# Three of the eleven down-projection units as seven block products each, with their sums and low parts on VectorE

## The chip, the cores and the metric

The kernel runs on one core of one Trainium2 chip. The metric is the device time of one execution in microseconds (us), as the median of several runs. The engines are TensorE (PE in the profile; PEld is its weight load), VectorE (DVE), ScalarE (ACT), GpSimd (POOL) and SyncE (SP), which issues most of the DMAs. SBUF is the working memory of all of them; PSUM (the tile `ps`, eight banks of 128x512) takes the matmul results and is read by ACT and DVE.

## What is computed

Two decoder layers on 256 tokens with a width of 1024. The change touches one product in each layer, that of the gated MLP with the down weights (2816x1024):

```
for i in range(DEPTH):                      # DEPTH = 2
    ...
    x = x + groups.reshape(B, S, MIX_WIDTH) @ w_o[i]
    h = rms_norm(x, ffn_norm[i])
    u = causal_depthwise_conv(h @ w_up[i], conv_w[i], conv_b[i])
    x = x + (jax.nn.silu(u[..., :D_FF]) * u[..., D_FF:]) @ w_down[i]
    x = x + (p[i] @ ple_proj[i]) * jax.nn.sigmoid(x @ ple_gate[i])
```

## The kernel before

**Split numbers.** Every large product is made from numbers split in two: a high part (the value rounded to the matmul format `fp32r` by a copy) and a low part (value minus high part). `split_product` (L963, L964, L965) issues three matmuls: high by high, high by low, low by high.

**Units.** The weights come as units of 128x2048 numbers (1 MB), some of half that. Each layer has 10 units of the input projection, 5 of `w_o`, one of `ple_proj`, 22 of `w_up`, 11 of `w_down` (`U_DOWN` + 0 to 10, here down 0 to down 10) and 5 of `ple_gate` (`U_GATE` + n, here gate 0 to 4). A unit passes through these steps, each engine doing its own in the order in which the code writes them:

- SP loads it into one of `DEEP` = 6 slots of `raw` when the unit six places earlier has been used (`w_used`, which PE raises after the last matmul of a unit).
- ACT copies it to the high part (`high`, L590) in one of `RING` = 3 buffers `wh`, when the unit three places earlier has been used.
- Someone subtracts the high part for the low part `wl`: POOL for everything from up unit 2 to the end of the layer (`low`, L461), DVE for the earlier ones (L1724).
- PE uses it, in the order of the units.

**The down stage.** The activation of step s (256 of the 2816 rows, so `STEPS` = 11 steps) is made during the up stage: DVE multiplies (`product`, L2082), ACT copies the high part (`product_high`, L894) and DVE subtracts (`product_low`, L2087) into `g_high(s)` and `g_low(s)`, which lie in `gT_h`, `gT_l` and `g_late`. For the two token tiles of 128 and the two halves of 512 columns, down unit s adds two products of depth 128 into one of the banks 0 to 3 (`wide`). That is 8 block products, or 24 matmuls of 128x512. When down 10 finishes a bank, `add_to_x` (L2041) on DVE adds the bank to one of the four quarters of `x` and signals `x_mlp`.

**After it.** PE waits for `x_mlp` quarter by quarter, transposes the quarter (`x_T`, L1015), ACT copies the high part (`x_high`, L604), DVE the low part (`x_low`, L1673), and PE begins gate 0 (L1539, L1541), whose first matmul waits for two of the four high parts. ACT makes the high parts of gate 0 and gate 1 before `x_high`, those of gate 2 to 4 after it; POOL makes their low parts.

A line of the profile is a line of the kernel; many lines belong to helpers.

Of the kernel before, what the change touches and what calls it, by code (L numbers as in the profile page):

```python
# [7 lines left out]
F32 = mybir.dt.float32  # L8
# [7 lines left out]
P = 128  # L16
# [40 lines left out]
DEEP = 6  # L57
# [18 lines left out]


def unit_up(s, half):

    return U_FFN + 2 * s + half  # L80
# [25 lines left out]
def _cols(n):  # L106
# [34 lines left out]
    "wo_done": 3, "x_mid": 4, "low_copied": 2 * STEPS, "halves_summed": 2 * STEPS, "tap2": 4 * STEPS, "tap1": 4 * STEPS, "conv_done": 4 * STEPS,  # L141
    "silu": STEPS, "prod": STEPS, "g_high": STEPS, "g_low": STEPS, 
    "proj_done": 3, "pp_ready": 4, "down_done": 3, "x_mlp": 4, "gate_ready": 3, "sigmoid": 4, "ple_term": 4,
# [30 lines left out]
def build(nc, x_in, p_cols, positions, w_in, w_uq, w_ukv, attn_cols, norm_gains,  # L174
          small_gains, w_o, w_up, conv_cols, w_down, ple_proj, ple_gate, out):
    with ExitStack() as ctx:
# [26 lines left out]
        with nc.sbuf_tensor("proj_h", [P, SLOT], F32R) as proj_h:  # L203
            pass
        hT = sb("hT", [P, KT, SEQ])
        hT_hl = sb("hT_hl", [P, KT * 2 * SEQ + UP_AT], F32R)
# [3 lines left out]
        sb("hT_edge", [P, 32])  # L210
        gT_h = sb("gT_h", [P, 2, 2, SEQ], F32R)
        gT_l = sb("gT_l", [P, 2, 2, SEQ], F32R)
# [19 lines left out]
        pT = sb("pT", [P, 2, SEQ])  # L232
        pT_h = sb("pT_h", [P, 2, SEQ], F32R)
        ng = sb("ng", [P, 2 * D])
        with nc.sbuf_tensor("uq_l", [P, 2, H * QK], F32R) as uq_l:
# [60 lines left out]
        def g_low(s):  # L296
            return gT_l[:, s] if s < EARLY else g_late[:, 1, s - EARLY]

        def mixed(high, g):
# [67 lines left out]
        def ffn_lows(layer, u):  # L367

            return layer * (UNITS - U_POOL) + (u + 1 - U_POOL)

# [47 lines left out]
        def _(pool):  # L418
# [36 lines left out]
            for layer in range(DEPTH):  # L455
# [101 lines left out]
                pool.wait_ge(F["hn_ready"], base["hn_ready"] + 4)  # L557
                for u in range(U_POOL, UNITS):
                    low(u)
# [6 lines left out]
        def _(act):  # L566
# [7 lines left out]
            for layer in range(DEPTH):  # L574
# [316 lines left out]
                def product_high(s):  # L891
# [3 lines left out]
                                   ).then_inc(F["g_high"], 1)  # L895

                act.wait_ge(F["conv_landed"], base["conv_landed"] + 16)
                high(U_FFN + 2)
                for s in range(STEPS):
                    low_half(s, 0)  # L900
                    high(unit_up(s, 0) + 3)
                    if s:
                        product_high(s - 1)
                    if s > 1:
                        act.wait_ge(F["g_low"], base["g_low"] + s - 1)
# [15 lines left out]
                if layer + 1 < DEPTH:  # L921
                    act.wait_ge(F["g_low"], base["g_low"] + STEPS)
                    latent_high(pt_r, M_MLA_B, layer + 1, "mla_high")
                    latent_high(pb_r, M_MLA_A, layer + 1, "mla_a_high")
# [14 lines left out]
        def _(pe):  # L939
# [6 lines left out]
            for layer in range(DEPTH):  # L946
                base = before(layer)
                def unit(u):

                    if u in WHOLE:  # L950
                        pe.wait_ge(raw_landed[u % DEEP],
                                   (layer * (UNITS // DEEP) + u // DEEP + 1) * 16)
                    elif u == U_WO:
                        pe.wait_ge(F["out_low"], layer + 1)
                    elif u < U_POOL:
                        pe.wait_ge(l_made, lows(layer, u))
                    else:
                        pe.wait_ge(ffn_l_made, ffn_lows(layer, u))
                    return u % DEEP, w_high(u)
# [565 lines left out]
                pe.wait_ge(F["conv_done"], base["conv_done"] + 4 * (STEPS - 1))  # L1525
                for s in range(STEPS):
                    pe.wait_ge(F["g_low"], base["g_low"] + s + 1)
                    wide(U_DOWN + s, 2, 0, g_high(s), g_low(s), s == 0, s == STEPS - 1,
                         name="down_done" if s == STEPS - 1 else None)
# [50 lines left out]
        def _(dve):  # L1580
# [64 lines left out]
            for layer in range(DEPTH):  # L1645
# [431 lines left out]
                def product(s):  # L2077

                    g = cv[s % 2][:, 0:2, :]
                    dve.wait_ge(F["silu"], base["silu"] + s + 1)  # L2080
                    dve.wait_ge(F["conv_done"], base["conv_done"] + s * 4 + 4)
                    tt(g, g, cv[s % 2][:, 2:4, :], ALU.mult).then_inc(F["prod"], 1)  # L2082

                def product_low(s):

                    dve.wait_ge(F["g_high"], base["g_high"] + s + 1)
                    tt(g_low(s), cv[s % 2][:, 0:2, :], g_high(s).bitcast(F32), ALU.subtract  # L2087
                       ).then_inc(F["g_low"], 1)

                dve.wait_ge(F["conv_landed"], base["conv_landed"] + 16)  # L2090
                for s in range(STEPS):
                    summed(s, 0)
                    if s:
                        product_low(s - 1)
# [4 lines left out]
                product_low(STEPS - 1)  # L2099


                add_to_x("down_done", U_GATE - 1, "x_mlp")
# [47 lines left out]
```

## Time and profile before

| What | us |
|---|---|
| Median of the runs shown (662.1, 662.16, 663.84) | 662.16 |
| Profiled execution, first to last instruction (its span) | 661.4 |
| PE busy in it | 653.2 |
| DVE busy in it | 441.5 |
| ACT busy in it | 420.2 |
| POOL busy in it | 402.8 |

The page gives no other time for the profiled execution than its span; the median of the runs is 0.76 us above that span, and that is taken as what lies around it. All times of rows below count from the start of the span. Start and duration of an instruction are printed; a row can stand for several merged instructions (x4). Behind a row stands in brackets how long the engine sat idle before it and who ended that.

### The profile page before, as it was taken

The numbers are of one execution on the slowest core, as the hardware profiler recorded it, in microseconds if no ns is written. First come the engines' busy times: TensorE is split into PE (matmuls) and PEld (weight loads), VectorE is DVE, ScalarE is ACT, GpSimd is POOL, SyncE is SP. The second block draws the span as 40 slices with busy tenths as digits, with TensorE's granted clock in tenths as the row PEclk, the third lists the DMA queues.
The fourth block names the chain that finished last, engine by engine and source line by source line (L and its number), as shares of the span: only waits on it lengthen the run. The fifth ranks groups of instructions, "written<-read, shape, count | busy, mean of one in ns | idle before, by whom it ended". The sixth has DMA issues, their size and how long they took to land.

```text
span 661.4 us, 9574 instructions
## 1 busy us (share of the span) xinstructions
PE 653.2 (99%) x3792; PEld 562.9 (85%) x3792; DVE 441.5 (67%) x637; ACT 420.2 (64%) x633; POOL 402.8 (61%) x212
## 2 busy tenths in 40 slices
PE   8999999999999999999999999999999999999997
PEld 6988887888888888888889879878888888888885
DVE  5997778758989985003488777875798989810033
ACT  6669886677767675334474879756777777733332
POOL 5443510288888887987841353005888888889871
PEclk9999999999999999999999999999999999999999
DMA  9972125675565555553387421165555555555411
GB/s 318 363 257 64 66 105 158 201 236 191 191 190 192 192 191 190 191 191 107 108 283 248 156 100 64 65 207 176 192 190 191 191 192 191 191 191 190 160 33 63
DMA packets 74606, 115.37 MB, mean 174 GB/s; under 512 B 2369, under 2 KB 58433, under 8 KB 74305
## 3 DMA queue, kind: packets, MB, share of 16 engines
q1 hardware_dynamic: 73408, 111.95, 50.8%
q10 hardware_dynamic: 1152, 2.81, 1.2%
q8 instruction: 30, 0.49, 0.3%
q14 instruction: 16, 0.12, 0.1%
HBM read 113.70 MB, written 1.05 MB: 174 GB/s over the span
## 4 chain that ended last, share of the span: by engine, by line
PE 95%; DVE 2%; DMA 1%; ACT 0%; issue 0%; SPq 0%; ACTq 0%
PE ps L1516 24%; PE ps L963 15%; PE ps L964 14%; PE ps L965 14%; PE ps L1518 12%; PE ps L1109 1%; PE ps L1015 1%; DMA raw<-w_in 1%; PE ps L1135 1%; PE ps L1375 1%; PE ps L977 1%; PE ps L1050 1%; PE ps L1147 1%; DVE hn L2110 1%; PE ps L1539 1%; PE ps L1541 1%
## 5 line engine op out<-in xcount | busy, mean ns | idle before, releaser
L461 POOL TENSOR_TENSOR wl<-raw,wh 128x2048 fp32r<-128x2048 f32 (+1 forms) x74 | 332.6, 4499 | 86.3 <-ACT wh L590 86.3
L1516 PE MATMUL ps<-hT_hl,wh 128*128 128x512 f32 x688 | 238.6, 392 | 0.0
L590 ACT ACTIVATE wh<-raw 128x2048 fp32r<-128x2048 f32 (+1 forms) x100 | 180.6, 1809 | 77.0 <-PE ps L965 69.4
L1518 PE MATMUL ps<-hT_hl,wl 128*128 128x256 f32 x688 | 193.3, 281 | 0.0
L1516 PEld LDWEIGHTS ps<-hT_hl,wh 128*128 128x128 f32 x688 | 129.1, 188 | 28.2
L1518 PEld LDWEIGHTS ps<-hT_hl,wl 128*128 128x128 f32 x688 | 129.4, 188 | 0.0
L963 PE MATMUL ps<-wh,hT_hl 128*128 128x512 f32 (+1 forms) x216 | 79.7, 369 | 0.0
L965 PE MATMUL ps<-wh,hT_hl 128*128 128x512 f32 (+1 forms) x216 | 77.4, 359 | 0.0
L964 PE MATMUL ps<-wl,hT_hl 128*128 128x512 f32 (+1 forms) x216 | 77.3, 358 | 0.0
L2041 DVE TENSOR_TENSOR x<-x,ps 128x512 f32<-128x512 f32 x16 | 10.8, 686 | 99.1 <-PE ps L965 98.7
L448 POOL TENSOR_SCALAR st<-st 128x2 f32<-128x2 f32 (+3 forms) x22 | 6.5, 295 | 114.6 <-ACT lat L665 62.2
L965 PE MATMUL ps<-wh,g_late 128*128 128x512 f32 x144 | 56.0, 389 | 0.0
L963 PE MATMUL ps<-wh,g_late 128*128 128x512 f32 x144 | 56.0, 389 | 0.0
L964 PE MATMUL ps<-wl,g_late 128*128 128x512 f32 x144 | 56.0, 389 | 0.0
L2074 DVE SCALAR_TENSOR_TENSOR pb<-ps,conv,pb 128x255 f32<-128x255 f32 (+1 forms) x96 | 39.5, 471 | 17.3 <-ACT pb L881 17.3
L1724 DVE TENSOR_TENSOR wl<-raw,wh 128x2048 fp32r<-128x2048 f32 (+1 forms) x24 | 48.2, 2017 | 0.1
L963 PEld LDWEIGHTS ps<-wh,hT_hl 128*128 128x128 f32 x216 | 40.8, 189 | 6.8 <-DVE wl L1724 0.7
L965 PEld LDWEIGHTS ps<-wh,hT_hl 128*128 128x128 f32 x216 | 40.7, 189 | 6.2
L964 PEld LDWEIGHTS ps<-wl,hT_hl 128*128 128x128 f32 x216 | 40.8, 189 | 5.4
L2087 DVE TENSOR_TENSOR g_late<-pb,g_late 128x512 fp32r<-128x512 f32 x10 | 38.4, 3843 | 3.8 <-ACT g_late L894 3.8
L2087 DVE TENSOR_TENSOR g_late<-pt,g_late 128x512 fp32r<-128x512 f32 x8 | 37.1, 4634 | 2.4 <-ACT g_late L894 2.4
L872 ACT ACTIVATE qk_moba<-ps 128x512 f32<-128x512 f32 x22 | 13.1, 598 | 38.7 <-PE ps L1518 38.7
(321 smaller groups left out, 1182.9 us busy)
## 6 DMA issues: line engine op xcount, KB each, us to landing
raw<-w_up SPq DMA_DIRECT2D x44, 1024.0 KB, 5.1
raw<-w_down SPq DMA_DIRECT2D x22, 1024.0 KB, 4.9
raw<-w_in SPq DMA_DIRECT2D x16, 1024.0 KB, 9.9
raw<-w_o SPq DMA_DIRECT2D x6, 1024.0 KB, 5.1
raw<-ple_gate SPq DMA_DIRECT2D x6, 1024.0 KB, 4.9
raw<-w_in SPq DMA_DIRECT2D x4, 704.0 KB, 5.6
ng<-norm_gains ACTq DMA_DIRECT2D x2, 1024.0 KB, 6.6
raw<-w_o SPq DMA_DIRECT2D x4, 512.0 KB, 3.9
```

The costliest lines, as they stand in the source:

```text
L461: pool.tensor_tensor(wl[:, slot, 0:n], raw[:, slot, 0:n], w_high(u)[:, 0:n].bitcast(F32), ALU.subtract).then_inc(done, 1)
L590: act.activation(w_high(u)[:, c:n], raw[:, slot, c:n], ACT.Copy).then_inc(h_made, 1)
L872: act.activation(low_halves[half], ps[:, bank:bank + 2, SEQ:2 * SEQ], ACT.Copy).then_inc(F["low_copied"], 1)
L963: pe.matmul(dst, a_h, b_h, start=start, stop=False, skip_group_check=True)
L964: pe.matmul(dst, a_h, b_l, start=False, stop=False, skip_group_check=True)
L965: return pe.matmul(dst, a_l, b_h, start=False, stop=stop, skip_group_check=True)
L1516: pe.matmul(both, high[:, c], hU_all[:, k].rearrange("p a n -> p (a n)"), start=k == 0, stop=False, skip_group_check=True)
L1518: mm = pe.matmul(o, wl[:, slot, c], hU_h[:, k, :], start=False, stop=k == KT - 1, skip_group_check=True)
L1724: tt(wl[:, slot, c:n], raw[:, slot, c:n], w_high(u)[:, c:n].bitcast(F32), ALU.subtract).then_inc(l_made, 1)
L2041: tt(x[:, t, c], x[:, t, c], ps[:, b, :], ALU.add).then_inc(F[done], 1)
L2074: stt(o, ps[:, bank + j, 0:SEQ - d], conv[:, tap, f:f + 1], o, ALU.mult, ALU.add).then_inc(F[name], 1)
L2087: tt(g_low(s), cv[s % 2][:, 0:2, :], g_high(s).bitcast(F32), ALU.subtract).then_inc(F["g_low"], 1)
```

## The change

`SEVEN` = (4, 6, 8): for these down units the 2x2 blocks of the activation (token tile by depth tile) and of the weights (depth tile by column half) are combined so that 7 block products do in place of 8 (`down_seven`). DVE makes four sums of activation blocks (`act_sums`) and four sums of weight blocks (`weight_sums`), ACT the high parts of what is new (`seven_high`), DVE the low parts (`act_rest`, `weight_rest`). Three of the seven products go straight into banks 1, 2 and 3, the other four gather over the three units in banks 4, 5, 6 and 7; after down 8 ACT copies banks 6 and 5 to SBUF (`both_sums`, `minus_both`, which lie in `qk_swa`), and eight additions on DVE bring the four banks to the quarters of `x`. The ordinary low parts of down 3 to 10 move from POOL to DVE (`down_low`). `product_high` and `product_low` of steps 4, 6 and 8 leave the up stage.

```diff
+SEVEN = (4, 6, 8)
+DVE_FROM = 3
@@ POOL
-                for u in range(U_POOL, UNITS):
+                for u in (*range(U_POOL, U_DOWN + DVE_FROM), *range(U_GATE, UNITS)):
                     low(u)
@@ ACT
+                def seven_high(i):
+                    u = U_DOWN + SEVEN[i]
...
+                    act.wait_ge(F["a_sums"], base["a_sums"] + i + 1)
+                    act.activation(a_high[:, i % 2, 0:3 * P], g_flat(SEVEN[i], True)[:, P:4 * P],
+                                   ACT.Copy)
+                    act.activation(a_high[:, i % 2, 3 * P:7 * P], g_flat(SEVEN[i], False), ACT.Copy
+                                   ).then_inc(F["a_rounded"], 1)
...
+                    act.wait_ge(F["w_sums"], base["w_sums"] + 4 * i + 4)
+                    act.activation(quarter_highs(i), quarters[:, i % 2], ACT.Copy
+                                   ).then_inc(F["w_rounded"], 1)
...
-                for u in range(U_DOWN + 3, U_GATE + 1):
-                    high(u)
+                for s in range(DVE_FROM, STEPS):
+                    if s in SEVEN:
+                        act.wait_ge(F["w_sums"], base["w_sums"] + 4 * SEVEN.index(s) + 2)
+                    high(U_DOWN + s)
+                    if s in SEVEN:
+                        seven_high(SEVEN.index(s))
+                act.wait_ge(F["sevens_done"], base["sevens_done"] + 1)
+                for o, bank in ((both_sums, 6), (minus_both, 5)):
+                    act.activation(o, ps[:, bank, :], ACT.Copy).then_inc(F["sevens_copied"], 1)
+                high(U_GATE)
                 high(U_GATE + 1)
                 x_high(8, AT_GATE)
@@ PE
+                    pe.wait_ge(F["a_rest"], base["a_rest"] + i + 1)
...
+                    product(4, a11, high, low, 1)
+                    product(3, a12, high, low, 3)
+                    product(2, s4, high, low, 2)
+                    product(5, s1, high, low, 0)
+                    pe.wait_ge(F["w_rest"], base["w_rest"] + i + 1)
+                    high, low = quarter_highs(i), quarter_sums(i)
+                    product(6, s2, high, low, 0)
+                    mm = product(7, s3, high, low, 1)
+                    if i == FEW - 1:
+                        mm.then_inc(F["sevens_done"], 1)
+                    product(1, a22, high, low, 2).then_inc(w_used, 1)
@@ DVE
+                def weight_sums(i):
...
+                    tt(t3, b12, b22, ALU.add).then_inc(F["w_sums"], 1)
+                    for n, (o, one, two) in enumerate(((b12, b12, b11), (t2, b12, b22),
+                                                       (t4, t2, b21))):
+                        tt(o, one, two, ALU.add).then_inc(F["w_sums"], 1)
+                        if n < 2:
+                            dve.wait_ge(F["w_sums"], base["w_sums"] + 4 * i + n + 2)
...
+                for s in range(DVE_FROM, STEPS):
+                    if s in SEVEN:
+                        weight_sums(SEVEN.index(s))
+                        act_sums(SEVEN.index(s))
+                    down_low(s)
+                    if s in SEVEN:
+                        act_rest(SEVEN.index(s))
+                        weight_rest(SEVEN.index(s))
+
+                dve.wait_ge(F["sevens_copied"], base["sevens_copied"] + 2)
+                parts = [x[:, t, c] for t, c in map(quarter, range(4))]
+                chained(tt(both_sums, both_sums, ps[:, 4, :], ALU.add))
+                chained(tt(minus_both, minus_both, both_sums, ALU.subtract))
+                tt(parts[2], parts[2], minus_both, ALU.add)
+                chained(tt(both_sums, both_sums, ps[:, 7, :], ALU.add))
+                chained(tt(parts[1], parts[1], both_sums, ALU.add))
+                chained(tt(minus_both, minus_both, ps[:, 7, :], ALU.subtract))
+                tt(parts[0], parts[0], minus_both, ALU.add)
+                chained(tt(parts[3], parts[3], ps[:, 4, :], ALU.add))
 
                 add_to_x("down_done", U_GATE - 1, "x_mlp")
```

`chained` makes DVE wait until the instruction that it wraps has ended.

On DVE, at the end of the down stage, there stood before the low part of the last activation step (L2087), the four additions of `add_to_x` (L2041) and `x_low` (L1673):

```order
L2087 TENSOR_TENSOR g_late<-pb,g_late 128x512 [waits g_high]
L2041 TENSOR_TENSOR x<-x,ps 128x512 [waits down_done] x3
L2041 TENSOR_TENSOR x<-x,ps 128x512 [waits w_used]
L1673 TENSOR_TENSOR hT_hl<-ps,hT_hl 128x4x128 [waits xT_high] x4
```

At the same place of the changed kernel's DVE, from the work of the last seven-product unit on, stand `weight_rest` (L2245), `down_low` of down 9 and 10 (L2253), the eight additions (L2267 to L2274) and then `add_to_x` (L2140):

```order
L2245 TENSOR_TENSOR hT_hl<-quarters,proj_h 128x1536 [waits w_rounded]
L2253 TENSOR_TENSOR wl<-raw,wh 128x2048 [waits h_made] x2
L2267 TENSOR_TENSOR qk_swa<-qk_swa,ps 128x512 [waits sevens_copied]
L2268 TENSOR_TENSOR qk_swa<-qk_swa 128x512 [waits dve_step]
L2269 TENSOR_TENSOR x<-x,qk_swa 128x512 [waits dve_step]
L2270 TENSOR_TENSOR qk_swa<-qk_swa,ps 128x512
L2271 TENSOR_TENSOR x<-x,qk_swa 128x512 [waits dve_step]
L2272 TENSOR_TENSOR qk_swa<-qk_swa,ps 128x512 [waits dve_step]
L2273 TENSOR_TENSOR x<-x,qk_swa 128x512 [waits dve_step]
L2274 TENSOR_TENSOR x<-x,ps 128x512
L2140 TENSOR_TENSOR x<-x,ps 128x512 [waits down_done,dve_step]
```

So the eight additions stand ahead of the first addition of `add_to_x`; four of them (L2268, L2269, L2271, L2273) have both inputs in SBUF, the other four have one in PSUM.

On ACT, at the same place of the changed kernel, stand the high parts of the last seven-product unit, down 9 and 10 (L625), the two copies out of PSUM (L974), the high parts of gate 0 and gate 1 (L625) and `x_high` (L639):

```order
L946 ACTIVATE proj_h<-quarters 128x1536 [waits w_sums]
L625 ACTIVATE wh<-raw 128x2048 [waits w_used,raw_landed5]
L625 ACTIVATE wh<-raw 128x2048 [waits w_used,raw_landed0]
L974 ACTIVATE qk_swa<-ps 128x512 [waits sevens_done]
L974 ACTIVATE qk_swa<-ps 128x512
L625 ACTIVATE wh<-raw 128x2048 [waits w_used,raw_landed1]
L625 ACTIVATE wh<-raw 128x2048 [waits w_used,raw_landed2]
L639 ACTIVATE hT_hl<-ps 128x4x128 [waits xT_ready] x4
```

Before, the rows of the high parts (L590 there) followed each other with nothing between; the two copies now stand between those of down 10 and gate 0.

## Rows read from the trace of the kernel before

**Rows 1.** The page, its parts 1 (busy time) and 2 (clock by slices).

```profile
PE 653.2 (99%) x3792; PEld 562.9 (85%) x3792; DVE 441.5 (67%) x637; ACT 420.2 (64%) x633; POOL 402.8 (61%) x212
PEclk9999999999999999999999999999999999999999
```

**Rows 2.** Timeline of the down stage, layer 0, PE: start, duration.

```profile
261.68 0.39 PE L963 MATMUL ps<-wh,g_late 128*128 128x512 f32 x1
261.91 0.39 PE L964 MATMUL ps<-wl,g_late 128*128 128x512 f32 x1
```

**Rows 3.** Timeline of ACT, the down stage of layer 0.

```profile
256.65 0.63 ACT L894 ACTIVATE g_late<-pb 128x512 fp32r<-128x512 f32 x1 [2.35 <-DVE pb L2082]
257.19 1.90 ACT L590 ACTIVATE wh<-raw 128x2048 fp32r<-128x2048 f32 x1
259.90 1.92 ACT L590 ACTIVATE wh<-raw 128x2048 fp32r<-128x2048 f32 x1 [0.81 <-PE ps L965]
...
297.98 1.92 ACT L590 ACTIVATE wh<-raw 128x2048 fp32r<-128x2048 f32 x1 [3.52 <-PE ps L965]
303.42 1.92 ACT L590 ACTIVATE wh<-raw 128x2048 fp32r<-128x2048 f32 x1 [3.52 <-PE ps L965]
```

**Rows 4.** Groups of DVE instructions by line and shape: busy us, mean ns, idle before.

```profile
L1724 DVE TENSOR_TENSOR wl<-raw,wh 128x2048 fp32r<-128x2048 f32 x18 | 41.0, 2284 | 0.1
L2041 DVE TENSOR_TENSOR x<-x,ps 128x512 f32<-128x512 f32 x16 | 10.8, 686 | 99.1 <-PE ps L965 98.7 <-PE ps L1375 0.5
```

**Rows 5.** Timeline of DVE at the end of layer 1: an instruction and the one chained to it.

```profile
651.42 0.69 DVE L2110 TENSOR_TENSOR hn<-pr,hn 128x512 f32<-128x512 f32 x1 [14.48 <-ACT hn L931]
652.15 0.69 DVE L2113 TENSOR_TENSOR x<-x,hn 128x512 f32<-128x512 f32 x1
```

**Rows 6.** Timeline of DVE, end of the up stage and beginning of the down stage.

```profile
213.15 4.63 DVE L2087 TENSOR_TENSOR g_late<-pb,g_late 128x512 fp32r<-128x512 f32 x1 [0.30 <-ACT g_late L894]
217.71 1.64 DVE L2074 SCALAR_TENSOR_TENSOR pt<-ps,conv,pt 128x255 f32<-128x255 f32 x4
219.27 0.68 DVE L2060 TENSOR_TENSOR ps<-ps,qk_moba 128x512 f32<-128x512 f32 x1
...
257.32 0.69 DVE L2087 TENSOR_TENSOR g_late<-pb,g_late 128x512 fp32r<-128x512 f32 x1 [0.70 <-ACT g_late L894]
```

**Rows 7.** Timeline of POOL, the same stretch and the end of the down stage.

```profile
212.61 4.62 POOL L461 TENSOR_TENSOR wl<-raw,wh 128x2048 fp32r<-128x2048 f32 x1 [0.92 <-ACT wh L590]
218.16 4.62 POOL L461 TENSOR_TENSOR wl<-raw,wh 128x2048 fp32r<-128x2048 f32 x1 [0.92 <-ACT wh L590]
...
251.44 4.63 POOL L461 TENSOR_TENSOR wl<-raw,wh 128x2048 fp32r<-128x2048 f32 x1 [0.91 <-ACT wh L590]
259.17 18.33 POOL L461 TENSOR_TENSOR wl<-raw,wh 128x2048 fp32r<-128x2048 f32 x4 [3.10 <-ACT wh L590]
```

**Rows 8.** Timeline of all engines, end of down 10 and beginning of gate 0.

```profile
308.61 1.91 PE L1015 MATMUL ps<-ident,x 128*128 128x128 f32 x16
308.80 0.69 DVE L2041 TENSOR_TENSOR x<-x,ps 128x512 f32<-128x512 f32 x1 [0.68 <-PE ps L965]
309.24 2.07 ACT L604 ACTIVATE hT_hl<-ps 128x512 fp32r<-128x512 f32 x4 [3.90 <-PE ps L1015]
310.27 0.48 PE L1539 MATMUL ps<-wh,hT_hl 128*128 128x512 f32 x1
```

**Rows 9.** Timeline of all engines, the end of layer 0.

```profile
322.47 1.36 ACT L611 ACTIVATE pt_r<-raw 128x1408 fp32r<-128x1408 f32 x1
...
322.64 2.41 POOL L461 TENSOR_TENSOR wl<-raw,wh 128x1024 fp32r<-128x1024 f32 x1 [2.49 <-ACT wh L590]
...
323.87 2.67 DVE L1680 TENSOR_TENSOR wl<-raw,pt_r 128x1408 fp32r<-128x1408 f32 x1 [11.51 <-ACT pt_r L611]
...
325.01 1.85 POOL L525 TENSOR_TENSOR gc<-rope_c,sg 128x128 f32<-128x128 f32 x1
```

**Rows 10.** Busy time by engine, granted clock (PEclk), DMA share of one stretch.

```profile
8.00:9.00 1.00, 0.31 (x1) 0.30 (x2) 1.00 (x3) 0.94 (x2) 0.86 (x3) 1.00 1.05 379
```

More of the change, by code:

```diff
@@ L75, with eights @@
 STEPS = FT // 2
+SEVEN = (4, 6, 8)
+FEW = len(SEVEN)
+DVE_FROM = 3
+def eights(s):
+    return s - sum(f < s for f in SEVEN)
 def unit_up(s, half):
@@ L205, in build @@
         hT = sb("hT", [P, KT, SEQ])
+        with nc.sbuf_tensor("quarters", [P, 2, 1536], F32) as quarters:
+            pass
         hT_hl = sb("hT_hl", [P, KT * 2 * SEQ + UP_AT], F32R)
@@ L1525, in _, with down_seven, product @@
                 pe.wait_ge(F["conv_done"], base["conv_done"] + 4 * (STEPS - 1))
+                def down_seven(i):
+                    s = SEVEN[i]
+                    slot, high = unit(U_DOWN + s)
+                    raw_a, sums_a = (g(s).rearrange("p k n -> p (k n)") for g in (g_high, g_low))
+                    rounded = a_high[:, i % 2]
+                    a = [(rounded[:, n * P:(n + 1) * P],
+                          raw_a[:, (n + 1) * P:(n + 2) * P] if n < 3 else
+                          sums_a[:, (n - 3) * P:(n - 2) * P]) for n in range(7)]
+                    a11, a22, a12, s1, s2, s3, s4 = a
+                    def product(bank, act, b_h, b_l, n):
+                        c = slice(n * 512, (n + 1) * 512)
+                        own = bank >= 4
+                        return split_product(ps[:, bank, :], *act, b_h[:, c], b_l[:, c],
+                                             own and i == 0, own and i == FEW - 1)
+                    pe.wait_ge(F["a_rest"], base["a_rest"] + i + 1)
+                    if i == 0:
+                        pe.wait_ge(F["conv_done"], base["conv_done"] + 4 * STEPS)
+                    low = wl[:, slot]
+                    product(4, a11, high, low, 1)
[9 more added lines that the diff above has]
+                    product(1, a22, high, low, 2).then_inc(w_used, 1)
                 for s in range(STEPS):
-                    pe.wait_ge(F["g_low"], base["g_low"] + s + 1)
+                    if s in SEVEN:
+                        down_seven(SEVEN.index(s))
+                        continue
+                    pe.wait_ge(F["g_low"], base["g_low"] + eights(s + 1))
                     wide(U_DOWN + s, 2, 0, g_high(s), g_low(s), s == 0, s == STEPS - 1,
@@ L2092, in _ @@
                     summed(s, 0)
-                    if s:
+                    if s and s - 1 not in SEVEN:
                         product_low(s - 1)
@@ new lines, in act_sums @@
+                def act_sums(i):
+                    dve.wait_ge(F["prod"], base["prod"] + SEVEN[i] + 1)
+                    a21, a11, a22, a12 = (g_flat(SEVEN[i], True)[:, n * P:(n + 1) * P]
+                                          for n in range(4))
+                    s1, s2, s3, s4 = (g_flat(SEVEN[i], False)[:, n * P:(n + 1) * P]
+                                      for n in range(4))
+                    chained(tt(s1, a21, a22, ALU.subtract))
+                    tt(s3, a11, a21, ALU.subtract)
+                    chained(tt(s2, s1, a11, ALU.subtract))
+                    tt(s4, a12, s2, ALU.add).then_inc(F["a_sums"], 1)
@@ new lines, in weight_rest, with down_low @@
+                def weight_rest(i):
+                    dve.wait_ge(F["w_rounded"], base["w_rounded"] + i + 1)
+                    o = quarter_sums(i)
+                    tt(o, quarters[:, i % 2], quarter_highs(i).bitcast(F32), ALU.subtract
+                       ).then_inc(F["w_rest"], 1)
+                def down_low(s):
+                    u = U_DOWN + s
+                    slot = u % DEEP
+                    dve.wait_ge(h_made, highs(layer, u))
+                    tt(wl[:, slot], raw[:, slot], w_high(u).bitcast(F32), ALU.subtract
+                       ).then_inc(F["down_low"], 1)
```

61 lines of the change are left out of this document (53 added, 8 removed).

## Prediction

> **What bounds the kernel now.** I first read the busy shares and the granted clock [rows 1]: PE is busy for 653.2 of 661.4 us, at full clock (2.4 GHz) in every slice. So what counts is PE's own work and any new wait in front of PE. In the down stage matmuls start 0.227 us apart [rows 2] although each row shows 0.39 us of duration: they overlap, and it is the distance that a removed matmul gives back. 24 of them make 5.44 us a unit, and ACT's rows confirm this: its next high part is let go by PE every 5.44 us (the last two of [rows 3]). I call E(u) the time at which down unit u ends on PE. ACT's high part of down 4 waits for down 1, so E(1) = 259.90 and, in steps of 5.44, E(3) = 270.78, E(8) = 297.98, E(9) = 303.42, E(10) = 308.86 (PE's rows put it at 308.80). Then I looked at where PE leaves the stage [rows 8]: transposes at 308.61, the last `add_to_x` at 308.80, first high part at 309.24, gate 0 at 310.27. That crossing costs little, because three of the four quarters of `x` are ready before E(10). Last I looked for who disturbs whom on DVE and POOL [rows 6, 7].
>
> **The collision that decides.** The same subtraction of 128x512 takes DVE 4.63 us at 213.15 and 0.69 us at 257.32 [rows 6]. At 213.15 POOL was in its own subtraction, from 212.61 to 217.23; DVE ended 0.55 us after that. At 257.32 POOL had been idle since 256.07 [rows 7]. So a DVE instruction with both inputs in SBUF waits until POOL's is over. With one input in PSUM it doesn't: at 219.27 DVE took 0.68 us while POOL worked from 218.16 to 222.78. And who waits gets the next turn: at 325.05 POOL's subtraction ended, DVE's waiting one ran on to 326.54, and POOL's next, of 128x128 only, shows 1.85 us because it had to wait in turn [rows 9].
>
> **The change, part by part.**
>
> *Matmuls.* Each of the three units loses one block product of 3 matmuls: 3 x 0.227 = 0.68 us, over two layers 18 x 0.227 = 4.1 us. That is the whole possible gain. The new E are: E(4) 275.54, E(5) 280.98, E(6) 285.74, E(7) 291.18, E(8) 295.94, E(9) 301.38, E(10) 306.82, so 2.04 us earlier at the end of the stage.
>
> *Work on DVE in the stage.* DVE had nothing to do there: behind its last subtraction, which ends at 258.0 [rows 6], it stood idle for PE until `add_to_x` (99.1 us over both layers [rows 4], nearly all of it here). A subtraction costs 2.28 us for 2048 columns and 0.69 for 512 [rows 4], so 1.04 ns a column and 0.15 us fixed; a following one that isn't chained starts some 0.08 us before the end [rows 6], a chained one 0.04 us after it [rows 5]. By this a seven-product unit takes: `weight_sums` 2.66, `act_sums` 1.04 (128 columns: 0.28 each), `down_low` 2.20, `act_rest` 1.07, `weight_rest` 1.66, together 8.6 us; an ordinary one 2.2. A pair takes 10.8 us against 5.44 + 4.76 = 10.2 on PE, so the lead melts. It begins with down 3 at 259.13, after ACT's high part [rows 3]. The activations of down 4 are ready at 268.4 (needed 270.78), of down 6 at 279.2 (280.98), of down 8 at 290.0 (291.18): spare times of 2.4, 1.8 and 1.2 us. The second weight set comes later but is needed 12 matmuls (2.7 us) later too. POOL has nothing to do from 256.07 to gate 0, so nothing slows these. I cost them at nothing on PE; if DVE were 4% slower over the 31 us before down 8, PE would wait there.
>
> *Work on ACT.* Per seven-product unit 384 + 512 + 1536 columns more, by rows of 0.63 us for 512 and 1.36 for 1408 about 2.5 us [rows 3, 9]. ACT sat idle 3.5 us in each 5.44. It waits for two of DVE's sums before the high part of such a unit, which is then made by 286.4 for down 8, just before DVE wants it at 286.8. No cost.
>
> *Loads, POOL, up stage.* SP's loads still wait for the unit six earlier and have the same size: that of down 8 is asked for at E(2) = 265.3 and wanted by its sums at 282.9, more than three units later. POOL loses eight subtractions a layer (18.33 us for four [rows 7]), which nobody waited for. The three dropped pairs of `product_high` and `product_low` shorten DVE's and ACT's up stage, where PE waits for neither: no gain.
>
> *The end of the stage.* Here I find the cost. The product into bank 7 of down 8 ends 3 matmuls before E(8), at 295.26. ACT's two copies (0.6 us each, overlapping a little) are done at 296.43. DVE is free at 296.1 and begins the eight additions at 296.47. ACT turns to the high part of gate 0, 1.92 us, and POOL can begin its low part at 298.4. DVE by then: L2267 to 297.2, L2268 to 297.9, L2269 from 297.9 to 298.6, ahead of POOL by 0.4 us. POOL gets its turn at 298.5 and holds until 303.1. L2270 has a PSUM input and runs; L2271 has not and waits until 303.1, ending 303.65. Meanwhile E(9) = 301.38 lets ACT make the high part of gate 1 until 303.3, so POOL waits with its next low part and takes its turn at 303.6, until 308.2. L2272 runs (to 304.4), L2273 waits and ends at 308.75, L2274 at 309.4. Only then come the four of `add_to_x`: 310.1, 310.7, 311.3, 311.9 are their ends.
>
> PE has been idle since 306.82. It transposes the first quarter from 310.14 to about 310.75 (before: 308.61 to 309.19), ACT's high parts of two quarters end at 311.97, and gate 0 starts at 312.0. Before it was 310.27. So each layer ends this crossing 1.75 us later than before: the 2.04 us of gain is spent and 1.75 us more. The other quarters (last high part 313.1) are needed at about 314.6, and the low parts of gate 1 and 2 also come in time (308.2; about 319.7 against 322.9). Behind it PE is as full as before, so nothing is given back.
>
> *Sum.* Layer 1 has the same code and stands alike: 2 x 1.75 = 3.5 us. 661.4 + 3.5 = 664.9 of span, and with the 0.76 us between span and median **665.7 us**, 0.5% slower. An error of 0.8 us a layer in this chain is easily possible: 664.1 to 667.3. About 0.3% (2 us) is what a measurement of this kernel can tell from no change.
>
> **A rule on the clock.** In this crossing PE would stand still for 3.3 us and then do only transposes for 1.9. The trace shows the clock at its upper level in all slices [rows 1], also where PE was busy for 0.31 of a us [rows 10]; it has no gap as long as the new one. By the rows the clock costs nothing. The Trainium skill, "TensorE: Matmul & The Clock Gate", Part 1, says that an idle TensorE falls to 1.2 GHz and comes back only after it has been kept busy; no run here shows this yet. By that rule the sum would have an extra that it doesn't have now.
>
> **The rivals.**
>
> 1. *The gain comes through (faster).* The four additions with both inputs in SBUF don't wait for POOL, or only one of them does. Place: L2271 and L2273. Then L2274 ends at about 302 (or 305.8 if only L2271 waits), `add_to_x` is done by 308.4 at the latest, and gate 0 starts 2.04 us earlier, or a little less: 662.16 - 4.1 = 658.1. It decides at whether L2273 is through before POOL's second turn, at 303.6. For it: additions into `x` from PSUM never waited [rows 4]. Against: those read PSUM, and all but the last subtraction of a layer that met POOL's took 4.63 us, as in [rows 6]. Chance 0.13.
>
> 2. *DVE is later, and an earlier addition is caught.* If DVE reaches L2269 0.4 us later, POOL goes first: L2269 ends at 303.5, L2271 at 308.65, the first `add_to_x` at 311.5, 1.3 us later than above. If L2268 is caught it is 2.7. DVE had 0.3 us to spare before the additions, so 0.7 us over a chain of 37 us is enough, and over 1.2 us PE would also wait in front of down 8. Two layers: 668.3 to 671.1. Chance 0.17.
>
> 3. *The clock falls after the gap.* No row has a matmul at 1.2 GHz, so I bound the price: nothing, or all of gate 0 at half rate, 24 x 0.227 = 5.44 us a layer, which gives 665.7 to 676.6. I take a quarter of the bound as its own value, since the gap is short beside what PE does around it: 668.4. It is the rule of the page named above worked out for this place. Chance 0.17.
>
> 4. *The crossing costs just what the units give* (660.2 to 664.1): if DVE wins one of the turns in one layer, or if my chain is 0.8 us too long in each. Chance 0.12.
>
> **How the numbers follow.** The main case, 665.7, has 0.41. Faster is rival 1: 0.13. Within 0.3% is rival 4: 0.12. The rest is slower: 0.75. The range leaves out rival 1, half of rival 4's lower part and the upper tails of rivals 2 and 3: 663.3 to 670.5. The main case alone is 664.1 to 667.3.
>
> **What would show it.** In the profile after: 21 matmuls 0.227 us apart in the three units; no PE wait inside the down stage; two of the eight additions a layer (L2271, L2273) at about 4 to 5 us, the other six at 0.7; PE idle for some 3.4 us before the transposes of L1077 with DVE's `x` as the releaser. If all eight take 0.7, rival 1 holds; if L2268 or L2269 is the long one, rival 2; if PEclk has a slice below 9 or the matmuls of gate 0 start 0.45 us apart, rival 3. The forecast is wrong at its root if DVE isn't held by POOL there.

## Result and profile after

The changed kernel took 669.5 us (median of 669.06, 669.39, 669.6 and 670.84), the kernel before 662.33 (median of four on the same chip). The ratio is 1.0109, with a 95% interval of 1.0095 to 1.0123: slower by 7.2 us. The forecast had the direction and the place, and its range held the time, but it said 3.5 us, half of the loss.

The page of the changed kernel, its busy times and its clock by slices, against [rows 1]:

```profile
PE 652.9 (98%) x3774; PEld 562.1 (84%) x3774; DVE 521.9 (78%) x729; ACT 432.9 (65%) x649; POOL 329.9 (49%) x196
PEclk9999999999999999998999999999999999999989
```

PE has the 18 matmuls less, and yet is busy as long as before. Two slices of the clock are below 9, where [rows 1] has none: they are the slices in which each layer goes from down to gate. The waits of PE say where it stood still (total us, times, longest):

```profile
PE ps L1077 <- DVE x L2140: 6.3, 2, 3.2
```

There is one new wait, once a layer, and nothing inside the down stage. The timeline of DVE at this place in layer 0 shows why `x` was late (start, duration):

```profile
296.14 0.69 DVE L2267 TENSOR_TENSOR qk_swa<-qk_swa,ps 128x512 f32<-128x512 f32 x1
296.87 0.69 DVE L2268 TENSOR_TENSOR qk_swa<-qk_swa 128x512 f32<-128x512 f32 x1
297.59 0.69 DVE L2269 TENSOR_TENSOR x<-x,qk_swa 128x512 f32<-128x512 f32 x1
298.20 0.68 DVE L2270 TENSOR_TENSOR qk_swa<-qk_swa,ps 128x512 f32<-128x512 f32 x1
298.92 4.39 DVE L2271 TENSOR_TENSOR x<-x,qk_swa 128x512 f32<-128x512 f32 x1
303.34 0.69 DVE L2272 TENSOR_TENSOR qk_swa<-qk_swa,ps 128x512 f32<-128x512 f32 x1
304.06 4.27 DVE L2273 TENSOR_TENSOR x<-x,qk_swa 128x512 f32<-128x512 f32 x1
308.25 0.68 DVE L2274 TENSOR_TENSOR x<-x,ps 128x512 f32<-128x512 f32 x1
308.96 2.48 DVE L2140 TENSOR_TENSOR x<-x,ps 128x512 f32<-128x512 f32 x4
```

And POOL in the same stretch:

```profile
298.00 4.76 POOL L496 TENSOR_TENSOR wl<-raw,wh 128x2048 fp32r<-128x2048 f32 x1 [42.11 <-ACT wh L625]
303.20 4.58 POOL L496 TENSOR_TENSOR wl<-raw,wh 128x2048 fp32r<-128x2048 f32 x1 [0.45 <-ACT wh L625]
```

Of the eight additions six take 0.7 us, and L2271 and L2273 take 4.4 and 4.3. Each began inside one of POOL's two subtractions and ended within 0.6 us of that subtraction's end, as in [rows 6, 7]. In layer 1 the same two rows are long (4.39 and 4.27). Next PE, the end of down 10 and the gate units:

```profile
306.16 0.39 PE L1027 MATMUL ps<-wh,g_late 128*128 128x512 f32 x1
309.70 3.42 PE L1077 MATMUL ps<-ident,x 128*128 128x128 f32 x16 [3.16 <-DVE x L2140]
312.77 0.78 PE L1638 MATMUL ps<-wh,hT_hl 128*128 128x512 f32 x1
313.35 0.45 PE L1640 MATMUL ps<-wl,hT_hl 128*128 128x512 f32 x1
318.67 0.39 PE L1025 MATMUL ps<-wh,hT_hl 128*128 128x512 f32 x1
```

The same four-block transposes took 1.91 us in [rows 8] and take 3.42 here, and the first matmul of gate 0 takes 0.78 us where it took 0.48. A part of this is that `add_to_x` hands over its quarters one by one until 311.44 (308.96 + 2.48). The windows of that stretch (us, busy time of PE, PEld, DVE, ACT, POOL, then the granted clock, the DMA share and GB/s) show the other part:

```profile
308.00:310.00 2.00, 0.30 (x3) 0.30 (x4) 1.97 (x4) 0.00 (x0) 0.00 (x0) 1.00 0.91 310
310.00:312.00 2.00, 2.00 (x12) 1.84 (x11) 2.00 (x4) 1.14 (x2) 0.00 (x0) 0.51 0.08 30
312.00:314.00 2.00, 2.00 (x10) 1.81 (x9) 1.64 (x4) 1.49 (x4) 0.00 (x0) 0.64 0.00 0
314.00:316.00 2.00, 2.00 (x11) 1.62 (x10) 0.48 (x1) 1.56 (x1) 0.36 (x1) 1.00 0.00 0
```

After the standstill the granted clock is 0.51, its lower level (1.2 GHz), and it is back at 1.00 in the window from 314. To measure the crossing as a whole I take the time from the start of down 10's last matmul to the first matmul of gate 1. Before, these two are the following rows of PE's timeline:

```profile
308.37 0.39 PE L965 MATMUL ps<-wh,g_late 128*128 128x512 f32 x1
...
315.81 0.39 PE L963 MATMUL ps<-wh,hT_hl 128*128 128x512 f32 x1
```

Before, the crossing took 7.44 us (308.37 to 315.81); after, 12.51 (306.16 to 318.67). That is 5.07 more, less the 2.04 a layer that the units gave, so 3.0 a layer and 6.1 in two (layer 1 has the same: 7.43 and 12.50); the spans differ by 5.9 (661.4 and 667.3).

### The profile page after: what moved, and what is told of

Same layout as the page of the kernel before. It is cut to its first block, busy times and chain, and to the rows that moved or that the text cites. A ratio compares the mean times of both kernels' runs of the same rounds, so it can differ in the third digit from the quotient of the medians.

```text
span 667.3 us, 9642 instructions
## 1 busy us (share of the span) xinstructions
PE 652.9 (98%) x3774; PEld 562.1 (84%) x3774; DVE 521.9 (78%) x729; ACT 432.9 (65%) x649; POOL 329.9 (49%) x196
## 4 chain that ended last, share of the span: by engine, by line
PE 90%; DVE 5%; issue 2%; DMA 1%; ACT 1%; SPq 0%; ACTq 0%
PE ps L1578 24%; PE ps L1025 13%; PE ps L1027 13%; PE ps L1026 13%; PE ps L1580 12%; PE ps L1077 2%; DVE x L2271 1%; DMA raw<-w_in 1%; PE ps L1171 1%; PE ps L1197 1%; PE ps L1437 1%; DVE wl L1779 1%; PE ps L1638 1%; PE ps L1112 1%; PE ps L1209 1%
## 5 line engine op out<-in xcount | busy, mean ns | idle before, releaser
L496 POOL TENSOR_TENSOR wl<-raw,wh 128x2048 fp32r<-128x2048 f32 (+1 forms) x58 | 259.2, 4470 | 165.8 <-ACT wh L625 165.8
L625 ACT ACTIVATE wh<-raw 128x2048 fp32r<-128x2048 f32 (+1 forms) x100 | 180.4, 1807 | 49.8 <-DVE raw L2214 23.6
L2173 DVE SCALAR_TENSOR_TENSOR pt<-ps,conv,pt 128x255 f32<-128x255 f32 (+1 forms) x80 | 33.0, 474 | 20.2 <-ACT pt L916 20.2
L1027 PE MATMUL ps<-wh,g_late 128*128 128x512 f32 x120 | 46.7, 389 | 0.0
L2253 DVE TENSOR_TENSOR wl<-raw,wh 128x2048 fp32r<-128x2048 f32 x16 | 36.4, 2286 | 2.2 <-ACT wh L625 2.2
L1025 PE MATMUL ps<-wh,g_late 128*128 128x512 f32 x96 | 37.3, 389 | 0.0
L1026 PE MATMUL ps<-wl,g_late 128*128 128x512 f32 x96 | 37.3, 389 | 0.0
```

The costliest lines, as they stand in the source:

```text
L496: pool.tensor_tensor(wl[:, slot, 0:n], raw[:, slot, 0:n], w_high(u)[:, 0:n].bitcast(F32), ALU.subtract).then_inc(done, 1)
L625: act.activation(w_high(u)[:, c:n], raw[:, slot, c:n], ACT.Copy).then_inc(h_made, 1)
L1025: pe.matmul(dst, a_h, b_h, start=start, stop=False, skip_group_check=True)
L1026: pe.matmul(dst, a_h, b_l, start=False, stop=False, skip_group_check=True)
L1027: return pe.matmul(dst, a_l, b_h, start=False, stop=stop, skip_group_check=True)
L2173: stt(o, ps[:, bank + j, 0:SEQ - d], conv[:, tap, f:f + 1], o, ALU.mult, ALU.add).then_inc(F[name], 1)
```

## The experiments

The theory after the result has three parts: the dropped matmuls give 4.1 us; the two held additions leave PE standing and cost more than that; and the standstill lowers the clock, which costs again. The rivals: that the seven-product work itself, or the low parts on DVE, is what costs; that only one of the two collisions matters; that the clock is a mere sign and costs nothing. The first four experiments share one set of runs of the kernel before (662.81 us).

### Both low parts of POOL wait for the additions

POOL takes up the low part of gate 0 when L2273 is done:

```diff
 # POOL
+                    if u == U_GATE:
+                        pool.wait_ge(F["sevens_added"], base["sevens_added"] + 1)
                     low(u)
...
 # DVE
-                tt(parts[0], parts[0], minus_both, ALU.add)
+                tt(parts[0], parts[0], minus_both, ALU.add).then_inc(F["sevens_added"], 1)
```

> The changed kernel, but GpSimd begins the low part of gate 0 only when the seventh of the eight additions on VectorE has ended. Theory L (two of the additions are held by GpSimd's subtractions; the clock then falls in the gap): all eight additions take 0.7 us and end at about 301.5 us in layer 0, ahead of the end of down 10; no gap on TensorE, no fall of the clock, the whole gain of 18 matmuls at 0.227 us comes through: 658.2 us, 0.6% faster than before. Rival W (the additions, or the other new work on VectorE, are too much whatever GpSimd does): still slower than before, 666 to 669 us. Rival M (a dropped matmul gives less than 0.227 us): no gap, but a time near 662.

Measured: 658.76 us, ratio 0.9939 (0.9927 to 0.9951), 4.05 us faster than before. DVE's additions (the lines stand two further down in this kernel):

```profile
297.99 0.69 DVE L2273 TENSOR_TENSOR x<-x,qk_swa 128x512 f32<-128x512 f32 x1
299.44 0.69 DVE L2275 TENSOR_TENSOR x<-x,qk_swa 128x512 f32<-128x512 f32 x1
301.65 0.69 DVE L2142 TENSOR_TENSOR x<-x,ps 128x512 f32<-128x512 f32 x1 [0.92 <-PE ps L1029]
```

POOL's two subtractions, of the same kernel:

```profile
300.21 9.21 POOL L496 TENSOR_TENSOR wl<-raw,wh 128x2048 fp32r<-128x2048 f32 x2 [45.24 <-DVE x L2275]
```

All eight take 0.7 us, and `add_to_x` now waits for PE, not PE for it. Counted from the end of ACT's high part of gate 0 (297.92 in the changed kernel, 296.99 here), POOL starts 3.1 us later, and PE doesn't notice. The crossing takes 7.43 us, as before the change. So the seven-product units give all of their 4.1 us, and nothing that DVE or ACT do for them costs PE anything.

### Only the second low part waits

Against the first experiment:

```diff
-                    if u == U_GATE:
+                    if u == U_GATE + 1:
                         pool.wait_ge(F["sevens_added"], base["sevens_added"] + 1)
```

> As the run before, but only the low part of gate 1 waits for the additions; that of gate 0 starts as in the changed kernel. Theory L: the first collision stays (the fifth addition some 4.4 us), the second goes (the seventh 0.7 us); the additions end at 305.8 us in layer 0, the first addition of the down banks at 306.4, just as down 10 ends; the loss is 0.2 to 0.4 us a layer: 658.5 to 659 us. Rival W: 666 to 669 us. If each collision costs the same, half of the way: about 664 us.

Measured: 659.16 us, ratio 0.9949 (0.9936 to 0.9963). DVE's additions that correspond to L2271 and L2273, and `add_to_x`:

```profile
298.34 4.39 DVE L2273 TENSOR_TENSOR x<-x,qk_swa 128x512 f32<-128x512 f32 x1
303.48 0.69 DVE L2275 TENSOR_TENSOR x<-x,qk_swa 128x512 f32<-128x512 f32 x1
304.81 2.48 DVE L2142 TENSOR_TENSOR x<-x,ps 128x512 f32<-128x512 f32 x4
```

The first collision is there at full length and the median is 0.4 us above the first experiment's, a difference within the noise; the profiled crossing is 0.3 us a layer longer (7.73 against 7.43). At 298 PE still had units 9 and 10 to do, and `add_to_x` starts at 304.8, about when PE ends down 10 (its last matmul starts at 305.58). It is the second, which starts when PE has 2.5 us of work left, that brings the loss. But the first sets it up: without the hold of L2271, L2273 would have run from about 300.4 to 301.1, ahead of POOL's second subtraction at 303.20. This is worked out from the rows of the changed kernel; no run takes away the first collision alone.

### The sums stay in PSUM

ACT copies a third bank, and the sums are written over banks 6 and 5, so that none of the eight additions has both inputs in SBUF. POOL is left as it is.

```diff
-                for o, bank in ((both_sums, 6), (minus_both, 5)):
+                for o, bank in ((both_sums, 6), (minus_both, 5), (bank_7, 7)):
...
-                chained(tt(both_sums, both_sums, ps[:, 4, :], ALU.add))
-                chained(tt(minus_both, minus_both, both_sums, ALU.subtract))
-                tt(parts[2], parts[2], minus_both, ALU.add)
...
+                minus, both = ps[:, 5, :], ps[:, 6, :]
+                chained(tt(both, both_sums, ps[:, 4, :], ALU.add))
+                chained(tt(minus, minus_both, both, ALU.subtract))
+                tt(parts[2], parts[2], minus, ALU.add)
...
```

> The changed kernel, but a third bank is copied by ScalarE and the sums are kept in PSUM, so that each of the eight additions has one input in PSUM and one in SBUF; GpSimd is left as it is. Theory L: no addition is held although GpSimd works at the same time; the eight take 5.6 us and end by 302.5 us in layer 0; 658.2 us. If GpSimd held VectorE by something other than the two SBUF inputs: two long additions again, 666 to 670 us. Rival W: 666 us or more.

Measured: 658.4 us, ratio 0.9935 (0.9923 to 0.9948). POOL's two subtractions, and below them, in DVE's timeline, two of the additions:

```profile
298.24 9.32 POOL L498 TENSOR_TENSOR wl<-raw,wh 128x2048 fp32r<-128x2048 f32 x2 [42.59 <-ACT wh L627]
```

```profile
299.18 0.69 DVE L2274 TENSOR_TENSOR x<-x,ps 128x512 f32<-128x512 f32 x1
300.64 0.69 DVE L2276 TENSOR_TENSOR x<-x,ps 128x512 f32<-128x512 f32 x1
```

Here POOL works at its old time and DVE's additions run beside it in 0.69 us. The two experiments take the collision away from opposite sides, one by the time, one by the place of the inputs, and both come out at the gain of the matmuls. That it is two SBUF inputs against POOL's subtraction, and not the order or the number of the additions, is thus shown.

### The standstill filled with matmuls

As the changed kernel, but PE does 14 matmuls into bank 6, which nobody reads any more, while it waits for `x`. The additions are held as before.

```diff
+                pe.wait_ge(F["sevens_copied"], base["sevens_copied"] + 2)
+                for _ in range(14):
+                    pe.matmul(ps[:, 6, :], g_high(STEPS - 1)[:, 0, 0:P],
...
                 x_T(x, AT_GATE, ("x_mlp", 0))
```

> The changed kernel with 14 matmuls of 128x512 more in each layer, into a bank that is free by then, between down 10 and the transposes: they take 3.2 us, as long as TensorE stood still there. The wait for the additions stays. Theory L: the clock stays at its upper level, the transposes and gate 0 run as before, and 1.5 us a layer come back: 666 to 666.5 us, faster than the changed kernel by 0.5%. If the clock costs nothing and the transposes were slow only because the quarters of x come one by one: 669.5 us as the changed kernel. If the added matmuls end later than the first quarter of x is ready: up to 0.3 us a layer more.

Measured: 666.71 us, ratio 1.0057 (1.0044 to 1.007). PE at the crossing:

```profile
306.56 3.33 PE L1631 MATMUL ps<-g_late 128*128 128x512 f32 x14
309.91 2.45 PE L1077 MATMUL ps<-ident,x 128*128 128x128 f32 x16
312.12 0.47 PE L1643 MATMUL ps<-wh,hT_hl 128*128 128x512 f32 x1
317.68 0.39 PE L1025 MATMUL ps<-wh,hT_hl 128*128 128x512 f32 x1
```

The window with the transposes:

```profile
310.00:312.00 2.00, 2.00 (x15) 1.46 (x16) 2.00 (x4) 1.40 (x3) 0.00 (x0) 1.00 0.15 56
```

The clock stays at 1.00, and PE, with 14 matmuls more in its way, is at gate 1 0.99 us earlier (317.68 against 318.67). The transposes, whose quarters come one by one here too, take 2.45 us, so of the 3.42 in the changed kernel up to 0.97 are the clock's. The kernel is 2.8 us faster than the changed one by the medians, 3.4 by the ratios. The crossing takes 11.34 us in both layers: 3.9 more than before by the wait for `x`, and the other 1.2 of the 5.07 a layer are the clock's.

### The low parts alone

The kernel before, with only one part of the change: the low parts of down 3 to 10 are DVE's.

```diff
-                for u in range(U_POOL, UNITS):
+                for u in (*range(U_POOL, U_DOWN + DVE_FROM), *range(U_GATE, UNITS)):
...
+                for s in range(DVE_FROM, STEPS):
+                    u = U_DOWN + s
...
+                    tt(wl[:, slot], raw[:, slot], w_high(u).bitcast(F32), ALU.subtract
+                       ).then_inc(F["down_low"], 1)
```

> The kernel before with one part of the change alone: the low parts of down 3 to 10 made by VectorE (2.3 us each) in place of GpSimd (4.6 us each); all units keep 8 block products. Theory L: nobody waited for these subtractions, and VectorE was idle there: the same as before, 662.3 us within 0.3%. Rival W (the new work on VectorE costs): slower.

Measured: 662.33 us (median of 11) against 662.17, ratio 1.0001 (0.9992 to 1.001). Its busy times:

```profile
PE 653.1 (99%) x3792; PEld 562.8 (85%) x3792; DVE 478.2 (72%) x653; ACT 420.1 (64%) x633; POOL 329.6 (50%) x196
```

73 us of work left POOL, DVE took on 37, and the time didn't move. By itself this part is worth nothing; the next run shows what it is for.

### The low parts left on POOL

The changed kernel, with the low parts of all down units on POOL, each of units 4, 6 and 8 after the four sums of its weights.

```diff
-                for u in (*range(U_POOL, U_DOWN + DVE_FROM), *range(U_GATE, UNITS)):
+                for u in range(U_POOL, UNITS):
+                    if u - U_DOWN in SEVEN:
+                        pool.wait_ge(F["w_sums"], base["w_sums"] + 4 * SEVEN.index(u - U_DOWN) + 4)
                     low(u)
...
-                    down_low(s)
```

> The changed kernel with the other part alone: seven block products in three units, but the low parts of down 3 to 10 stay with GpSimd, which waits for the weight sums where it must. Theory L: the eleven additions and subtractions of each seven-product unit on VectorE, all with both inputs in SBUF, now meet GpSimd's subtractions in the middle of the down stage; served in turn the two engines need some 15 us for a pair of units in which TensorE needs 10.2; TensorE waits for units 4, 6 and 8, by 15 to 40 us over both layers: 684 to 709 us. Rival W: VectorE has 17 us less work in the stage, so it would be faster than the changed kernel, below 669 us.

Measured: 711.41 us, ratio 1.073 (1.0714 to 1.0747). The largest waits of PE, then three rows of DVE and two of POOL:

```profile
PE ps L1023 <- DVE g_late L2236: 15.8, 4, 4.0
PE ps L1075 <- DVE x L2138: 13.2, 2, 6.6
```

```profile
265.35 4.59 DVE L2224 TENSOR_TENSOR g_plain<-g_plain 128x128 f32<-128x128 f32 x1
...
274.62 0.69 DVE L2209 TENSOR_TENSOR quarters<-raw 128x512 f32<-128x512 f32 x1
275.23 5.05 DVE L2212 TENSOR_TENSOR raw<-raw 128x512 f32<-128x512 f32 x1
```

```profile
265.19 4.60 POOL L495 TENSOR_TENSOR wl<-raw,wh 128x2048 fp32r<-128x2048 f32 x1 [1.36 <-DVE quarters L2212]
274.80 4.92 POOL L495 TENSOR_TENSOR wl<-raw,wh 128x2048 fp32r<-128x2048 f32 x1 [5.01 <-ACT wh L626]
```

An addition of 128 columns, 0.28 us when it is free, takes 4.59 us: what is lost goes by how much of POOL's subtraction is left, not by the size of what waits. It goes the other way as well: POOL's subtraction that began at 274.80, while DVE's addition from 274.62 was running, shows 4.92 us in place of 4.60. The time is 2 us above what I had allowed. As they stand, the seven-product units need the low parts moved out of POOL: the prediction noted that an idle POOL slows nothing there, but put no figure to it, and it is worth some 42 us (711.4 against 669.5). These 42 us are not the collisions alone: POOL also waits for the sums of the weights there, and the mean granted clock is 0.98 against 0.993 in the changed kernel; no run parts the three.

### The standstill without the collision, whole, filled and half filled

To have the clock apart from the additions, three kernels build on the first experiment (nothing is held) and let PE wait for the low part of gate 1 ahead of the transposes: with nothing in the wait, with 14 matmuls in it (as in the diff), and with 8. They share one set of runs of the kernel before (662.28 us).

```diff
+                pe.wait_ge(F["sevens_copied"], base["sevens_copied"] + 2)
+                for _ in range(14):
+                    pe.matmul(ps[:, 6, :], g_high(STEPS - 1)[:, 0, 0:P],
...
+                pe.wait_ge(ffn_l_made, ffn_lows(layer, U_GATE + 1))
                 x_T(x, AT_GATE, ("x_mlp", 0))
```

> The run e1_pool_waits (no collision, all quarters of x ready when down 10 ends) with one wait more: TensorE starts the transposes only when GpSimd has ended the low part of gate 1, at about 309.4 us in layer 0, so that it stands still for 3.6 us in each layer although nothing on VectorE is late. Theory C (a standstill of this length takes the clock down, and that costs 1.2 to 1.6 us a layer by itself): 658.8 + 7.2 + 2.4 to 3.2 = 668.4 to 669.2 us, PEclk near 0.5 over the transposes, which then start 0.2 us apart although x is all there. Rival N (the slow transposes of the changed kernel came from the quarters of x arriving one by one): 658.8 + 7.2 = 666.0 us with PEclk at 1.00.

> The run e7_gap_alone with 14 matmuls of 128x512 (3.2 us) in the standstill of each layer; the transposes start at the same time as there. Both theories: 666.0 us, clock 1.00 throughout; theory C then has e7_gap_alone slower than this by 2.4 to 3.2 us, rival N by nothing.

> As e8_gap_filled with 8 matmuls in place of 14, so that TensorE works on for 1.8 us and then stands still for 1.8 us. If any standstill takes the clock down: between e7_gap_alone and e8_gap_filled, about 667.5 us. If one of this length doesn't: 666.0 us as e8_gap_filled, clock 1.00.

Measured: 670.03 us with nothing in the wait (ratio 1.0112, 1.0098 to 1.0126), 666.28 with 14 matmuls (1.0057, 1.0043 to 1.0071) and 668.88 with 8 (1.0096, 1.0083 to 1.011). The first is 0.8 us above the upper end that the theory of the clock gave for it, and 4 above the rival. With nothing in the wait, PE's timeline and three windows:

```profile
309.71 3.67 PE L1079 MATMUL ps<-ident,x 128*128 128x128 f32 x16 [3.75 <-POOL wl L496]
313.04 0.78 PE L1641 MATMUL ps<-wh,hT_hl 128*128 128x512 f32 x1
```

```profile
308.00:310.00 2.00, 0.29 (x2) 0.29 (x3) 0.00 (x0) 0.00 (x0) 1.66 (x1) 0.50 0.80 295
310.00:312.00 2.00, 2.00 (x11) 2.00 (x10) 0.51 (x1) 0.88 (x2) 0.00 (x0) 0.50 0.00 0
...
638.00:640.00 2.00, 1.29 (x8) 1.29 (x9) 0.00 (x0) 0.44 (x1) 0.66 (x1) 0.77 0.00 0
```

The window of 310 to 312 with 14 matmuls in the wait:

```profile
310.00:312.00 2.00, 1.98 (x17) 1.99 (x18) 0.66 (x2) 1.29 (x3) 0.00 (x0) 1.00 0.00 1
```

A wait for another engine and another reason takes the clock down just so, and the same wait with PE kept busy doesn't: 3.75 us between two kernels whose transposes start within 0.3 us of each other. So it is PE's standing still that lowers the clock, and the clock that costs. What one fall costs differs. The profiled crossings are 13.87 and 13.06 us with nothing in the wait, 11.49 and 11.50 with 14 matmuls: 2.4 us in layer 0, where the clock was down before the transposes began, and 1.6 in layer 1, where it fell after they had begun (638.71). Together that is 3.9, close to the 3.75 of the medians. With 8 matmuls in the wait PE stood still for 1.98 us in both layers:

```profile
310.13 1.97 PE L1079 MATMUL ps<-ident,x 128*128 128x128 f32 x16 [1.98 <-POOL wl L496]
...
636.75 3.19 PE L1079 MATMUL ps<-ident,x 128*128 128x128 f32 x16 [1.98 <-POOL wl L496]
```

The granted clock in a window of each layer:

```profile
310.00:312.00 2.00, 1.86 (x17) 1.87 (x18) 0.54 (x1) 1.17 (x3) 0.08 (x1) 1.00 0.02 6
638.00:640.00 2.00, 2.00 (x11) 2.00 (x10) 1.63 (x3) 1.26 (x4) 0.00 (x0) 0.50 0.00 0
```

In layer 0 the clock stayed up (crossing 11.46 us), in layer 1 it fell (13.09). Why the one and not the other is open; no run here tells it. The median is above what either theory gave for this kernel, and nearer to the one by which the clock falls.

## Why the prediction was half right

**Where the time went.** By the ratios, in parts of 662 us: the matmuls give 4.0 (first experiment, -0.61%); the held additions with a full clock take 7.8 (from 0.9939 to 1.0057); the lower clock takes 3.4 (from 1.0057 to 1.0109). The sum is 7.2. By the intervals of the ratios the first is good to 0.8 us, and the other two, each a difference of two ratios, to about 1.2. The profiled crossings of both layers give the same 7.8 for the held additions (2 x 3.90), and 2.3 for the clock (2 x 1.17), so the clock's term stands at 2.3 to 3.4 us. The 3.75 of the last group is of a kernel whose clock fell earlier in one layer, and is no measure of this one.

**Matmuls: right.** Forecast 4.1 us, measured 4.05. The start-to-start distance, not the duration of a row, was the right price.

**DVE and ACT inside the stage: right.** Costed at nothing on PE; the trace shows no wait there, and the first experiment gets the full gain. The activations of the three units were ready in time, although the DVE chain had a lead of only 1.2 us by my working: those of down 8, forecast for 290.0, were done at 289.95.

**The end of the stage: right, to a few tenths.** Forecast and trace for layer 0: L2271 ends at 303.65 and 303.3; POOL's second turn starts at 303.6 and 303.2; L2273 ends at 308.75 and 308.3; the first transpose starts at 310.14 and 309.70. The forecast had gate 0 1.75 us later than before, so gate 1 at 315.81 + 1.75 = 317.56; the kernel with the filled standstill has it at 317.68, and its time is 3.9 us above before where the forecast had 3.5. It was also as forecast that POOL goes ahead of L2271 and then of L2273. The forecast let POOL wait for L2271's end before its second turn, and this trace doesn't show such a wait: POOL's row names ACT's high part as what let it start at 303.20. The Trainium skill, "SBUF — State Buffer", section "Who interferes with whom", says that a VectorE instruction with two SBUF inputs contends with a GpSimd instruction that reads SBUF, and that the order of issue decides which of the two blocks. The trace agrees: POOL's subtractions began first, and the additions took 4.39 and 4.27 us against 0.69, and 0.69 again with one input in PSUM.

**The step that failed: the rule on the clock.** "By the rows the clock costs nothing" was the term of the main case, on the ground that no row of before had the clock down; I had written in the sentence before that before has no gap as long as the new one, so those rows couldn't bear it. With the main case's own mechanism came its own standstill (3.3 us forecast, 3.16 shown), and the clock fell in both layers. This was rival 3, put beside the main case at 0.17 as though it were another way for things to go, when it was a term to be added once the main case holds. What it does, the runs show: 16 transposes in 3.42 us in place of the 2.45 with the clock up, gate 0's first rows slow, 1.2 us a layer by the profiled crossings and 1.7 by the ratios, against nothing in the main case and 1.35 in rival 3's own value (668.4, which is 1.1 below the time). That this value came so near is luck: it was a quarter of a bound and not worked out from the transposes, which are most of it. The Trainium skill, "TensorE: Matmul & The Clock Gate", Part 1, says that an idle TensorE falls to 1.2 GHz; the granted clock of 0.51 behind the gap agrees.

**What lies around the span.** The forecast took 0.76 us, the difference between the median and the profiled span of before. The profiled run of the changed kernel has its own time, 669.06, beside its span of 667.3: 1.76 us, and the first experiment has 657.98 beside 656.2. So the profiled execution of before (661.4) belongs to a run of about 663.1, 0.8 us above its median, and that of after is 0.4 below its own. This is why the spans differ by 5.9 us and the medians by 7.2. It doesn't move the forecast, which added its 3.5 us to the median.

**The other rivals.** Rival 1 did not happen in the changed kernel, but it is what the first and the third experiment make of it: 658.1 forecast, 658.76 and 658.4 measured. Its condition ("whether L2273 is through before POOL's second turn") is just what the second experiment shows, with some 0.4 us for the first collision alone. Rival 2 is excluded: L2268 and L2269 take 0.69 us. Rival 4 is excluded by the filled standstill, which is 0.57% slower with the clock up.

## What to carry to other kernels

Before adding small VectorE instructions ahead of a point at which TensorE waits, look at what GpSimd does at that moment: if both inputs lie in SBUF, each instruction can be held for the whole of a GpSimd subtraction (4.6 us here), whatever its own size; one operand in PSUM, or one semaphore that lets GpSimd start 3 us later, turned 1.1% slower into 0.6% faster. When a forecast says that TensorE will stand still for some 2 us or more in a place where it never did (the clock fell after 1.98 us in one of two layers), put the price of the clock into the sum and not among the rivals: rows of a trace without such a gap say nothing about it. Where the time of the profiled run is known, compare that with its span before comparing spans with medians.

## What the runs showed of the hardware

- TensorE's clock fell to half during or right after a standstill of 3.2 us (the changed kernel) and 3.75 (with nothing in the wait), in both layers of each, and stayed up after one of 0.66. After standstills of 1.98 us in one kernel it stayed up in one layer and fell in the other.
- A fall has no fixed price. By the profiled crossings it cost 1.2 us in each layer of the changed kernel, 2.4 and 1.6 with nothing in the wait, and 1.6 in layer 1 with 8 matmuls in it. In layer 0 of the changed kernel the clock is back at 1.00 in the window from 314, with gate 0 under way.
- A VectorE instruction with two SBUF inputs and GpSimd's subtraction wait for each other in both directions: GpSimd's of 274.80 in the run with the low parts left on it took 4.92 us in place of 4.60, behind a VectorE addition begun at 274.62, and VectorE's next, begun at 275.23, took 5.05. A VectorE addition of 128 columns was held as long (4.59 us) as one of 512 (4.39).
